# Attention and the last stage in one region, with five output blocks moved into the last stage's first slots

## Chip, core and metric
The kernel runs on one core of one Trainium2 chip. The metric is the device time of one execution in microseconds (us). Five engines with a queue each work side by side and meet at semaphores: TensorE (PE; PEld are its weight loads), VectorE (DVE), ScalarE (ACT), GpSimd (POOL) and SyncE (SP), which issues most transfers. TensorE writes its products into PSUM, eight banks of 128 x 512 floats, which the other engines empty.

## What is computed
One inference step of a decoder layer with three groups of heads, for a prompt of 1024 tokens and 8 sequences of 4 new tokens (32 rows). All is float32. Cut to what matters:

```python
def mix_out(x, a, b, c, w_out, g_post):
    hcat = concatenate([a, b, c])              # 1024 + 512 + 512 columns
    return x + rmsnorm(hcat @ w_out, g_post)

def layer(...):
    pp = split(rmsnorm(x_p, g_pre) @ w_in)
    a_p, pC, pn, pm = mlstm_branch(pp, ...)    # chunks in order, state C, n, m carried on
    b_p = sparse_attention(pp)                 # 256 keys per query, softmax, * silu(z)
    c_p = memory_attention(pp)                 # 256 memory tokens, softmax, * silu(z)
    y_p = mix_out(x_p, a_p, b_p, c_p, w_out, g_post)
    # the same for the 32 decode rows, with caches and an mLSTM state per sequence
```

The output projection `hcat @ w_out` is split by rows of `w_out`: the half of groups B and C (rows 1024 to 2047) is computed in the attention stage and stored as a partial result, the half of group A is added in the last stage.

## The kernel before
The program is four stages in order (`build`): `project_index`, `select`, `attend_bc` and `mix_out`. Each runs through `Program.run`: a region (`nc.Block`) in which each engine has its own hand-written instruction list, closed by a barrier of all engines, and then a short region in which SyncE clears the stage's semaphores.

`attend_bc` runs over units, one per tile of 128 tokens (8) and head (4): 32 units, `A_UNITS`, unit `s` in slot `s`. A slot holds the scores of one unit, the softmax of it on VectorE and ScalarE, the transposed weights and the product with the values of the unit before. Six slots behind (`A_LAG`) come the output blocks: group `n` is one of the four blocks of 512 columns of tile `n // 4` of the B and C half, eight products of 128 x 512 accumulated in the one bank `at_bank_bc` (`multiply`, L2113, its first four products ahead of `turn_h`, its last four behind). ScalarE copies the bank to SBUF (`evacuate`, L2272), SyncE stores it to `y_part` (L1963). With 32 units and a lag of 6 the slots run to 38: in slots 34 to 37 there is only a group (28 to 31) in each. After them come 32 products for the decode rows (L2211), their copy and their store (L2000). SyncE asks in slot 33 for what the last stage begins with (gate rows, decode queries and keys, units 0 and 1), in slot 34 for two blocks of `w_out` and unit 2, in slot 35 for unit 3.

`mix_out` first turns gate rows into columns (L3133), decode queries and keys (L3150), and forms the decode dots (L3157). Then slots -2 to 36 follow, one per unit (chunk of 128 tokens and head, 32 in all). In slot `s` TensorE turns the keys of unit `s + 2` (L3044), forms the dots of `s + 1` (L3054), turns the output of `s - 1` (L3090), works on a decode step (L3118, every fourth slot L3125), then the numerator of unit `s` (L3066, L3068) and its key-value products (L3079). Between these stand, five slots behind (`LAG`), two halves of four products each of an output block of group A (`multiply`, L3093; products L3105). Dots and numerator share a bank, so the dots of a unit wait until VectorE has read the numerator before (`output`, L2702); that needs a square on ScalarE (L2881) and a root on GpSimd (L2968, L2971). `w_out` blocks 2 and 3 of the A half are requested by GpSimd in slot 0 (L2989). Units are loaded by SyncE four slots ahead (`units.load`, six requests), each when the unit before it in its buffer is used up.

## Time and profile before

| | us |
|---|---|
| median of 3 runs (2821.35 to 2826.67) | 2823.8 |
| profiled execution | 2823.03 |
| its span, first to last instruction | 2821.2 |
| TensorE busy | 2722.3 (96%) |
| VectorE, ScalarE, GpSimd busy | 1249.4, 579.0, 404.7 |
| mean granted clock of TensorE | 0.985 of full |
| end of the last decode product of attention | 2407.9 |
| first instruction of the last stage on TensorE | 2411.7 |
| first output product of group A | 2471.0 |

Times in the trace count from the start of the span. A timeline row is a run of equal instructions of one engine in order of time; in brackets stands how long the engine idled before it and what ended that. A float32 product of TensorE leaves two records (a block of eight products reads x16). The end of a matmul is modelled, so rows of TensorE overlap by a few tenths; distances are taken from start to start. A table of stretches gives the busy time of each engine in a window, the mean granted clock (1.00 is 2.4 GHz, 0.50 is 1.2 GHz), the mean busy share of the DMA engines and what they moved. "DMA to landing" is the time from a request to its arrival.

### The profile page before, as it was taken

What the parts mean: (1) busy time and instruction counts of PE and PEld (TensorE: products, weight loads), DVE (VectorE), ACT (ScalarE), POOL (GpSimd) and SP (SyncE); (2) the same over time, 40 slices, a digit from 0 to 9 for tenths busy, and PEclk for the clock granted to TensorE, in tenths of its full rate; (3) what the DMA queues carried; (4) which work ended last, traced back from release to release, by engine and by line L of the source; (5) the groups of instructions that cost most, each with busy time, mean ns of one, the idle gap of its engine ahead of it and who ended that gap; (6) DMA issues with size and microseconds to landing.
All of it is one profiled execution on the core that took longest, in us unless ns stands there. A gap on an engine that the chain in (4) does not pass through costs nothing. (4 is left out here: it accounts for less than half of the span.)

```text
span 2821.2 us, 35962 instructions
## 1 busy us (share of the span) xinstructions
PE 2722.3 (96%) x13915; PEld 1935.7 (69%) x13915; DVE 1249.4 (44%) x2147; ACT 579.0 (21%) x1367; POOL 404.7 (14%) x819
## 2 busy tenths in 40 slices
PE   8998999999999999999999999999699999699998
PEld 6674468846844588888888888888455564455553
DVE  3252588767754572142222245441322331345453
ACT  3123458660000000000011100110222231122121
POOL 0000013320000000000000033220133100334332
PEclk9999999999999999999999999999899999799999
DMA  6458212211322221222332255443945214665652
GB/s 228 103 158 269 84 36 72 84 44 59 103 75 84 68 79 43 74 83 85 105 122 76 84 179 158 136 137 113 306 142 155 79 47 136 206 198 178 209 156 99
DMA packets 273463, 342.00 MB, mean 121 GB/s; under 512 B 40989, under 2 KB 226325, under 8 KB 268013
## 3 DMA queue, kind: packets, MB, share of 16 engines
q1 hardware_dynamic: 239932, 262.65, 29.7%
q0 software_dynamic: 16288, 67.46, 7.6%
q10 hardware_dynamic: 17072, 9.58, 1.1%
q8 instruction: 112, 1.84, 0.3%
q14 instruction: 59, 0.48, 0.1%
HBM read 262.16 MB, written 80.01 MB: 121 GB/s over the span
## 5 line engine op out<-in xcount | busy, mean ns | idle before, releaser
L1396 PE MATMUL sbank<-w,xT 128*128 128x256 f32 x3200 | 698.6, 379 | 0.0
L1396 PEld LDWEIGHTS sbank<-w,xT 128*128 128x128 f32 x3200 | 606.5, 190 | 85.0 <-issue 3.3
L1396 PE MATMUL sbank<-w,area 128*128 128x256 f32 x1664 | 361.3, 379 | 0.0
L1815 DVE TENSOR_TENSOR pout_b<-pout_b,sbank 128x256 f32<-128x256 f32 x320 | 134.3, 421 | 503.4 <-PE sbank L1396 414.7
L1396 PEld LDWEIGHTS sbank<-w,area 128*128 128x128 f32 x1664 | 315.9, 190 | 42.8
L1778 DVE TENSOR_TENSOR w<-w 128x2048 f32<-128x2048 f32 x63 | 142.9, 2289 | 320.6 <-PE sbank L1396 257.4
L2121 PE MATMUL at_bank_bc<-w,at_hT 128*128 128x512 f32 x512 | 229.9, 593 | 3.9 <-ACT at_bc_out L2276 3.9
L1488 ACT ACTIVATE pout_b<-sbank 128x256 f32<-128x256 f32 x120 | 45.1, 382 | 890.6 <-PE sbank L1396 658.3
L1396 PE MATMUL sbank<-w 128*128 128x256 f32 x832 | 181.8, 379 | 2.6 <-issue 2.6
L1396 PEld LDWEIGHTS sbank<-w 128*128 128x128 f32 x832 | 158.0, 190 | 24.2 <-issue 2.8
L1393 PE MATMUL sbank<-xT,w 128*128 128x512 f32 x384 | 166.6, 593 | 0.0
L2121 PEld LDWEIGHTS at_bank_bc<-w,at_hT 128*128 128x128 f32 x512 | 94.6, 190 | 103.0 <-issue 101.6
L1393 PEld LDWEIGHTS sbank<-xT,w 128*128 128x128 f32 x384 | 72.7, 190 | 90.1 <-issue 90.0
L3105 PE MATMUL mo_bank_acc<-area,w 128*128 128x512 f32 x256 | 116.2, 598 | 0.0
L3105 PE MATMUL mo_bank_acc<-w 128*128 128x512 f32 x256 | 116.2, 598 | 0.0
L1512 ACT ACTIVATE pout_b<-pout_b 128x256 f32<-128x256 f32 x72 | 30.0, 417 | 358.9 <-DVE pout_b L1815 358.9
L2012 POOL DMA_INDIRECT at_vg<-in_cache_v,rowid x64 | 60.5, 945 | 277.6 <-PE at_bank_dec L2174 148.3
L1393 PE MATMUL sbank<-area,w 128*128 128x512 f32 x192 | 82.9, 592 | 0.0
L3105 PEld LDWEIGHTS mo_bank_acc<-area,w 128*128 128x128 f32 x256 | 46.4, 190 | 52.6 <-issue 52.6
L3105 PEld LDWEIGHTS mo_bank_acc<-w 128*128 128x128 f32 x256 | 46.5, 190 | 52.1 <-issue 52.0
L1596 DVE MAX8 m8s<-decode_scores 128x8 f32<-128x2052 f32 x32 | 73.4, 2294 | 0.1
L1599 DVE FIND_INDEX8 c8s<-m8s,decode_scores 128x8 uint32<-128x2052 f32 x32 | 73.3, 2291 | 0.0
(446 smaller groups left out, 3295.7 us busy)
## 6 DMA issues: line engine op xcount, KB each, us to landing
w<-in_w_in SPq DMA_DIRECT2D x64, 1024.0 KB, 5.1
proj<-pout_b SPq DMA_DIRECT2D x208, 128.0 KB, 1.7
area<-in_x_prompt SPq DMA_DIRECT2D x16, 1024.0 KB, 7.6
attention_then_units<-proj SPq DMA_DIRECT2D x128, 128.0 KB, 2.6
area<-roped_q_of_decode POOLq DMA_DIRECT2D x32, 256.0 KB, 4.1
w<-in_w_out SPq DMA_DIRECT2D x4, 2048.0 KB, 15.5
y_of_groups_b_c<-at_bc_out SPq DMA_DIRECT2D x32, 256.0 KB, 2.3
mo_dec_states<-in_state_mlstm_C SPq DMA_DIRECT2D x32, 256.0 KB, 6.4
```

The lines of the kernel that those rows point to most:

```text
L1393: last = nc.tensor.matmul(bank[2 * u][:, :], at[name][:, c, P * u:P * (u + 1)], x(c, 0, SEQ // 2), start=first_ and c == 0, stop=c == 7, s ...
L1396: last = nc.tensor.matmul(bank[t][:, 0:256], x(c, t * P, (t + 1) * P), at[name][:, c, :], start=first_ and c == 0, stop=c == 7, skip_group ...
L1488: nc.scalar.activation(out[:, t, :], product_at(n, t), function if kind else ACT.Copy).then_inc(first_read, 1)
L1512: nc.scalar.activation(qout[:, t, :], qout[:, t, :], function).then_inc(shaped, 1)
L1596: order.step(nc.vector.max(m8s[:], ss[:]))
L1599: order.step(nc.vector.max_index(c8s[:], m8s[:], ss[:]))
L1778: nc.vector.tensor_tensor(quarter[out], quarter[x], quarter[y], op).then_inc(w_sums, 1)
L1815: nc.vector.tensor_tensor(out[:, t, :], x[:, t, :], product_at(n, t), ALU.add).then_inc(sums_read, 1)
L2012: nc.gpsimd.indirect_dma_start(out=vg[:, 4 * (q % 2) + g, :], out_offset=None, in_=ins["cache_v"][:, :], in_offset=bass.IndirectOffsetOnAx ...
L2121: last = nc.tensor.matmul(acc[:, :], hT[:, t % 2, j, :], w[:, j, b * O_W:(b + 1) * O_W], start=j == 0, stop=j == HT - 1)
L3105: last = nc.tensor.matmul(acc[n % 2][:, :], hT[:, c % 2, j, :], w[b][:, j, :], start=j == 0, stop=j == HT - 1)
```

## The change
Attention and the last stage run in one region, `run_joined`. Each engine goes from its attention list straight on to its list of the last stage, where it first waits for one semaphore, `attention_over` (`over`). SyncE raises it after its last wait of attention and after clearing attention's semaphores. The semaphores that both stages use are kept in the program's outer list.

Attention keeps 28 groups (`BC_OWN`), the tiles 0 to 6. The last of them goes into the bank `at_bank_dots0` instead of the shared one. The five blocks that are left (`BC_CARRIED`): the decode block (`None`) and block 3 of tile 7 stand at the end of attention's list, into the banks `kept_bank1` and `kept_bank0`; blocks 2, 0 and 1 of tile 7 come in slots -1 and 0, 1 and 2, 3 and 4 of the last stage, two products ahead of and two behind the dots of a slot (`carry`). The kept banks are the later banks of the A half. ScalarE copies the carried blocks (`copy_carried`), SyncE stores them (`store_carried`), with waits for the landing of the store that used the buffer before.

For that, the transposed outputs of odd tiles, of the decode rows and the two output buffers live over both stages; `w_out` lies in four separate blocks; gate columns and decode dots go to the bank `th`; the normalizer of the decode rows is asked for by attention; the load of `w_out` block 0 and 1 and of units 2 and 3 moves behind the start of the last stage; GpSimd's blocks 2 and 3 move to slots 3 and 5, since they overwrite the B and C half.

```diff
+    def run_joined(self, first, second):
+        with ExitStack() as second_stage:
+            with self.nc.Block() as joined:
+                with ExitStack() as self.stage:
+                    self.in_stage = []
+                    first(self, joined)
+                self.stage, self.in_stage = second_stage, []
+                second(self, joined)
...
+BC_OWN = A_UNITS - O_B
+BC_CARRIED = (None, O_B - 1, 2, 0, 1)
...
-        slots = range(A_UNITS + A_LAG)
+        slots = range(A_UNITS + 2)
+        def out_bank(n):
+            return qs0 if n == BC_OWN - 1 else acc
...
         @block.sync     # attention
-                if s == A_UNITS + 2:
-                    for b in range(2):
-                        sp.dma_start(k.w_a(b), ins["w_out"][0:ML_W, b * O_W:(b + 1) * O_W].rearrange("(c p) n -> p c n", p=P)
-                                     ).then_inc(k.w_a_in[b], 16)
-                    units.load(sp, 2)
-                if s == A_UNITS + 3:
-                    units.load(sp, 3)
-            n = A_UNITS - 1
+            n = BC_OWN - 1
             sp.wait_ge(evacuated, n + 1)
-            sp.wait_ge(evacuated, A_UNITS + 1)
-            sp.dma_start(k.y_part_dec[:, :], out[:, 0, :]).then_inc(y_out[0], 16)
-            sp.wait_ge(y_out[0], 16 * (A_UNITS // 2 + 1))
-            sp.wait_ge(y_out[1], 16 * (A_UNITS // 2))
+            k.clear(sp)
+            sp.sem_inc(k.attention_over, 1)
...
         @block.tensor   # attention
-                    if n:
+                    if n == BC_OWN - 1:
+                        pe.wait_ge(read, A_UNITS)
+                    elif n:
                         pe.wait_ge(evacuated, n)
...
-            pe.wait_ge(evacuated, A_UNITS)
+            pe.wait_ge(evacuated, BC_OWN - 1)
             for c in range(HT):
                 for b in range(O_B):
...
+            pe.wait_ge(h_kept, A_UNITS)
+            b = BC_CARRIED[1]
+            for j in range(HT):
+                last = nc.tensor.matmul(ov[:, :], k.hT_odd[:, j, :], w[b][:, j, :], start=j == 0, stop=j == HT - 1)
...
         @block.sync     # last stage
+            def store_carried(i):
+                b = BC_CARRIED[i]
+                sp.wait_ge(bc_copied, copied(i))
+                sp.dma_start(k.y_part_dec[:, :] if b is None else k.y_part[SEQ - P:SEQ, O_W * b:O_W * (b + 1)],
+                             k.out_parts[:, i % 2, :]).then_inc(y_part_out[i % 2], 16)
...
+            units.load(sp, 2)
+            store_carried(0)
+            for j in range(ML_H):
+                load_states(j)
+            units.load(sp, 3)
+            load_w(0)
+            store_carried(1)
+            load_w(1)
+            for j in range(ML_H, 8):
+                load_states(j)
             for s in slots:
+                if s in (1, 3, 5):
+                    store_carried(2 + s // 2)
...
         @block.scalar   # last stage
+            def copy_carried(i):
+                act.wait_ge(bc_done, copied(i))
+                act.wait_ge(y_part_out[i % 2], 16 * (BC_OWN + i) // 2 if i % 2 == 0 else 16 * (BC_OWN + i - 1) // 2)
+                nc.scalar.activation(k.out_parts[:, i % 2, :], carried_bank(i)[:, :], ACT.Copy).then_inc(bc_copied, 1)
...
+                if s == -2:
+                    copy_carried(1)
+                if s in (0, 2, 4):
+                    copy_carried(2 + s // 2)
...
         @block.gpsimd   # last stage
-                if s == 0:
-                    for b in range(2, O_B):
+                if s in (3, 5):
+                    b = 2 + s // 5
+                    pool.wait_ge(bc_done, copied(b + 1))
...
         @block.tensor   # last stage
+            def carry(s, part):
+                i, first = carried(s), 4 * ((s + 1) % 2) + 2 * part
+                if first == 0:
+                    pe.wait_ge(bc_copied, copied(i - 2))
+                for j in range(first, first + 2):
+                    last = nc.tensor.matmul(carried_bank(i)[:, :], k.hT_odd[:, j, :], w_bc[BC_CARRIED[i]][:, j, :],
+                                            start=j == 0, stop=j == HT - 1)
+                if first == HT - 2:
+                    last.then_inc(bc_done, 1)
```

What stands in TensorE's list at the junction, before. `at_hT` are the turned head outputs, `at_dec_hT` those of the decode rows, 32 x 512 their products.

```order
L2121 MATMUL at_bank_bc<-w,at_hT 128x512 x8
L2133 MATMUL at_bank_turn<-ident_sb,at_ho 128x128 x2
L2121 MATMUL at_bank_bc<-w,at_hT 128x512 x36
L2211 MATMUL at_bank_bc<-w,at_dec_hT 32x512 x32
L1864 UNCONDITIONAL_BRANCH
L3037 UNCONDITIONAL_BRANCH
```

And now, with both banks called `kept_bank`.

```order
L2154 MATMUL kept_bank<-w,at_hT_of_even_tiles 128x512 x4
L2154 MATMUL at_bank_dots<-w,at_hT_of_even_tiles 128x512 x4
L2166 MATMUL at_bank_turn<-ident_sb,at_ho 128x128 x2
L2154 MATMUL at_bank_dots<-w,at_hT_of_even_tiles 128x512 x4
L2244 MATMUL kept_bank<-w,dec_hT 32x512 x32
L2250 MATMUL kept_bank<-w,hT_of_odd_tiles 128x512 x8
L3134 UNCONDITIONAL_BRANCH
```

The 36 products in a row (half of group 27, then groups 28 to 31) are gone from in front of the decode block; eight of them stand behind it, and one branch to the next list is left of two.

The opening of the last stage on TensorE, from the decode dots to the turn after the first numerator, before.

```order
L3157 MATMUL mo_bank_acc<-mo_dec_qT,mo_dec_kT 32x32 x8
L3054 MATMUL mo_bank_dots_num<-attention_then_units,mo_kT 128x128 x2
L3044 MATMUL mo_bank_turn_qk<-ident_sb,attention_then_units 128x128 x2
L3054 MATMUL mo_bank_dots_num<-attention_then_units,mo_kT 128x128 x2
L3066 MATMUL mo_bank_dots_num<-attention_then_units,mo_sd 128x257
L3068 MATMUL mo_bank_dots_num<-mo_state,mo_qs 128x257 x2
L3079 MATMUL mo_bank_kv<-attention_then_units,mo_kw 128x257 x2
L3196 MATMUL mo_bank_dec_num<-mo_dec_v,mo_dec_sd 32x257 x4
L3044 MATMUL mo_bank_turn_qk<-ident_sb,attention_then_units 128x128 x2
```

And now, `hT_of_odd_tiles` being the carried operand.

```order
L3262 MATMUL mo_bank_turn_h<-mo_dec_qT,mo_dec_kT 32x32 x8
L3210 MATMUL kept_bank<-w,hT_of_odd_tiles 128x512 x2
L3151 MATMUL mo_bank_dots_num<-attention_then_units,mo_kT 128x128 x2
L3210 MATMUL kept_bank<-w,hT_of_odd_tiles 128x512 x2
L3141 MATMUL mo_bank_turn_qk<-ident_sb,attention_then_units 128x128 x2
L3210 MATMUL kept_bank<-w,hT_of_odd_tiles 128x512 x2
L3151 MATMUL mo_bank_dots_num<-attention_then_units,mo_kT 128x128 x2
L3210 MATMUL kept_bank<-w,hT_of_odd_tiles 128x512 x2
L3163 MATMUL mo_bank_dots_num<-attention_then_units,mo_sd 128x257
L3165 MATMUL mo_bank_dots_num<-mo_state,mo_qs 128x257 x2
L3176 MATMUL mo_bank_kv<-attention_then_units,mo_kw 128x257 x2
L3305 MATMUL mo_bank_dec_num<-mo_dec_v,mo_dec_sd 32x257 x4
L3141 MATMUL mo_bank_turn_qk<-ident_sb,attention_then_units 128x128 x2
```

Four pairs of products of the first carried block came in around the dots (L3054, now L3151), all ahead of the first numerator (L3066, now L3163).

SyncE's list before, from the store of group 27 on: the `w_out` blocks and unit 2.

```order
L2485 DMA attention_then_units<-gate_rows 128x2x128
L1963 DMA y_of_groups_b_c<-at_bc_out 128x512
L1991 DMA area<-in_w_out 128x8x512 x2
L2480 DMA attention_then_units<-mlstm_queries_turned 128x2x128
L2483 DMA attention_then_units<-proj 128x256 x3
L2484 DMA attention_then_units<-proj 128x256
L2485 DMA attention_then_units<-gate_rows 128x2x128
```

And now, from the last request of unit 1 on (the ISA row are the clears, with the release right behind them).

```order
L2522 DMA attention_then_units<-gate_rows 128x2x128
L130 ISA x9
L2032 DMA y_of_groups_b_c<-out_parts 128x512
L2630 UNCONDITIONAL_BRANCH
L2648 DMA mo_dec_rows_everywhere<-gate_rows 128x8x32
L2650 DMA mo_decay_everywhere<-gate_decay 128x64
L2652 DMA mo_dec_mask<-in_dec_causal 32x32
L2654 DMA mo_dec_row_of<-in_dec_row_of 32x8 x2
L2656 DMA mo_dec_v<-proj 32x4x256 x2
```

The release stands ahead of the constants, and no block of `w_out` stands in front of them; these follow behind unit 3.

## Rows read from the trace of the kernel before

**Rows 1.** Page, part 2: granted TensorE clock in tenths, 40 equal slices of the span.
```profile
PEclk9999999999999999999999999999899999799999
```

**Rows 2.** Table of stretches: window, length, busy PE, PEld, DVE, ACT, POOL; clock, DMA, GB/s.
```profile
2407.90:2428.40 20.50, 8.00 (x59) 6.27 (x59) 9.49 (x25) 3.35 (x12) 8.12 (x16) 0.62 0.60 173
2428.40:2449.10 20.70, 14.85 (x68) 9.33 (x68) 7.23 (x23) 3.64 (x11) 8.02 (x17) 0.75 0.98 346
2449.10:2471.00 21.90, 17.95 (x59) 13.16 (x58) 11.25 (x40) 3.92 (x12) 5.89 (x13) 0.66 0.61 184
...
2480.40:2534.90 54.50, 54.50 (x207) 30.88 (x206) 27.85 (x79) 11.71 (x35) 21.33 (x36) 1.00 0.64 186
```

**Rows 3.** Timeline of TensorE: start, length, line, operation, output<-inputs, count, [idle before <-releaser].
```profile
2364.88 3.60 PE L2121 MATMUL at_bank_bc<-w,at_hT 128*128 128x512 f32 x8
2369.26 7.11 PE L2121 MATMUL at_bank_bc<-w,at_hT 128*128 128x512 f32 x16 [0.78 <-ACT at_bc_out L2276]
...
2400.79 7.07 PE L2211 MATMUL at_bank_bc<-w,at_dec_hT 128*32 128x512 f32 x64 [0.78 <-ACT at_bc_out L2276]
2411.74 0.66 PE L3133 MATMUL mo_bank_acc<-ident_sb,attention_then_units 12*128 12x12 f32 x9 [3.88 <-PEq L113]
```

**Rows 4.** Timeline of VectorE, same columns.
```profile
2412.20 1.77 DVE L2770 MEMSET mo_state<- 128x2056 f32 x1 [54.81 <-PEq L113]
...
2420.23 0.42 DVE L2680 TENSOR_TENSOR mo_qs<-attention_then_units 128x256 f32<-128x256 f32 x1 [3.80 <-DMA mo_dec_row_of<-in_dec_row_of]
...
2422.21 0.28 DVE L2689 SCALAR_TENSOR_TENSOR mo_sd<-mo_bank_dots_num,mo_dt 128x128 f32<-128x128 f32 x1
...
2456.45 0.29 DVE L2689 SCALAR_TENSOR_TENSOR mo_sd<-mo_bank_dots_num,mo_dt 128x128 f32<-128x128 f32 x1 [0.54 <-PE mo_bank_dots_num L3054]
```

**Rows 5.** Timeline of TensorE, opening and first slots of the last stage.
```profile
2416.48 1.06 PE L3157 MATMUL mo_bank_acc<-mo_dec_qT,mo_dec_kT 128*32 128x32 f32 x16 [0.23 <-DVE mo_dec_kT L2783]
...
2428.43 1.20 PE L3066 MATMUL mo_bank_dots_num<-attention_then_units,mo_sd 128*128 128x257 f32 x2 [4.61 <-DVE mo_sd L2689]
...
2446.46 0.44 PE L3044 MATMUL mo_bank_turn_qk<-ident_sb,attention_then_units 128*128 128x128 f32 x2 [4.88 <-DMA attention_then_units<-gate_rows]
...
2450.16 1.92 PE L3068 MATMUL mo_bank_dots_num<-mo_state,mo_qs 128*128 128x257 f32 x4
...
2455.73 0.68 PE L3054 MATMUL mo_bank_dots_num<-attention_then_units,mo_kT 128*128 128x128 f32 x4 [1.68 <-DVE mo_a L2709]
...
2470.99 3.60 PE L3105 MATMUL mo_bank_acc<-area,w 128*128 128x512 f32 x8
...
2475.81 1.08 PE L3125 MATMUL mo_bank_dec_num<-mo_dec_states,mo_dec_q_slot 128*32 128x257 f32 x16
```

**Rows 6.** Timeline of SyncE's requests (SPq) at attention's end.
```profile
2368.49 0.43 SPq L2485 DMA_DIRECT2D attention_then_units<-gate_rows  x1
...
2370.87 7.23 SPq L2480 DMA_DIRECT2D attention_then_units<-mlstm_queries_turned  x1
```

**Rows 7.** Timeline of TensorE, one steady slot.
```profile
2480.36 0.60 PE L3066 MATMUL mo_bank_dots_num<-attention_then_units,mo_sd 128*128 128x257 f32 x2
2480.79 1.03 PE L3068 MATMUL mo_bank_dots_num<-mo_state,mo_qs 128*128 128x257 f32 x4
...
2482.74 3.60 PE L3105 MATMUL mo_bank_acc<-area,w 128*128 128x512 f32 x8
2486.18 0.61 PE L3054 MATMUL mo_bank_dots_num<-attention_then_units,mo_kT 128*128 128x128 f32 x4
...
2487.57 3.70 PE L3105 MATMUL mo_bank_acc<-area,w 128*128 128x512 f32 x8
2491.11 0.60 PE L3066 MATMUL mo_bank_dots_num<-attention_then_units,mo_sd 128*128 128x257 f32 x2
```

**Rows 8.** Landing: w_out blocks (page, part 6, median), gate_rows in 2340 to 2480.
```profile
w<-in_w_out SPq DMA_DIRECT2D x4, 2048.0 KB, 15.5
...
DMA to landing us min/median/max: 3.5/5.3/11.0
```

More of the change, by code:

```diff
@@ L2489, with mix_out @@
 DEC = DEC_B * ML_H
-def mix_out(k):
+def mix_out(k, block):
     nc, ins, outs = k.nc, k.ins, k.outs
@@ L3128, in decode @@
                     last.then_inc(d_num, 1)
+            pe.wait_ge(over, 1)
             pe.wait_ge(rows_in, 16)
@@ L3162, in _ @@
                     multiply(group(s), 0)
+                if carried(s) is not None:
+                    carry(s, 0)
                 if -1 <= s and s + 1 < UNITS:
@@ L3188, in _ @@
                     multiply(group(s), 1)
+                if carried(s) is not None:
+                    carry(s, 1)
                 if 0 <= s < UNITS:
```

141 lines of the change are left out of this document (92 added, 49 removed).

## The prediction

> **What bounds the kernel now.** I read the 40 slices of the page first. TensorE's granted clock is 9 tenths or more but for two slices, of which the second covers 2398 to 2468 us [rows 1]; it lies at the junction that the change touches. The stages are serial, so what is gained at a junction comes off the end. The table of stretches sizes the dip [rows 2]: from 2407.9 to 2471.0 TensorE is busy 40.8 of 63.1 us at a mean clock of 0.62 to 0.75, so much of that busy time is itself time at 1.2 GHz. From 2480.4 to 2534.9 it is never idle, at full clock.
>
> The timeline of TensorE shows what stands there [rows 3]. The last tile's four output blocks of eight products run alone: 7.11 us each (16 records stand for 8 products, 0.86 us a product), each after a gap of 0.78 in which ScalarE empties the single bank. The decode block of 7.07 follows, then 3.88 of nothing at the barrier. VectorE does nothing meanwhile: its first work comes after 54.8 us of idling [rows 4]. Once the last stage has begun, its first numerator product starts only at 2428.43, 16.7 after TensorE came back [rows 5]. That is a latency chain: the constants land at 2420.2, only then does VectorE go on, and it takes 8.2 more. The next slots are again waits on the other engines, plus one of 4.88 for a unit's rows, with the products between them at half speed. The filler (the blocks) stands before the hole instead of in it.
>
> **Part 1: attention's end.** Group 27 goes to a bank of its own, so one gap of 0.78 goes: its second half starts at 2364.1 instead of 2364.88 and is through 3.44 later, at 2367.5. The decode block follows (7.1, to 2374.6), then block 3 of the last tile into the second kept bank (7.1, to 2381.7), without a gap, since that bank is free. Before, this point lay at 2407.87. Three blocks are put off, and a wait on one semaphore replaces the barrier.
>
> **Part 2: does TensorE find the semaphore raised?** SyncE raises it behind the last tile's requests and the two first units, which are issued by 2368.9 [rows 6]. The decode normalizer adds an issue (as the others, 0.43), and the copy of group 27 that SyncE waits for is over at about 2368.4. Nine clearing instructions follow. The whole restart in the trace, with seven of them, two barriers and a store's landing, is 3.88, so the release lies between 2369.3 and 2373.2; I take 2370.3. All of it is before 2381.7, the time TensorE gets there. From then on VectorE's fill of 1.77, the constants and GpSimd's first tables run under the decode block and block 3. The constants took from 2411.74 to 2420.23, 8.5: they are there by 2379, or by 2381.7 at the late end, still ahead of their first use at about 2388. The two w_out blocks of 2 MB and units 2 and 3 are moved behind the release; in the trace the issue right behind those blocks took 7.23 [rows 6]. That jam moves to about 2386 and ends before unit 4 is asked for at about 2398.
>
> TensorE's jump to the next code takes something between 0 and the 3.88 of the restart. I take 0.6, near the lower end, since the 3.88 also holds landing, barriers and clears. The Trainium skill (Runtime: NRT & Kernel Launch, Instruction fetch mechanics) has a rule against it: a taken branch to code that isn't at hand must fetch before execution goes on. By it the sum would lose up to 3.3 more; the trace holds such a jump in the same 3.88 and shows none by itself.
>
> **Part 3: the opening.** TensorE starts at 2382.3. In the trace it needs 4.74 from its first transposes to the decode dots (2411.74 to 2416.48) and 1.06 for these [rows 3, 5], which gives 2388.1. The first quarter of a carried block (two products, 1.72) ends at 2389.8. From the start of a unit's dots to VectorE's weights are 0.72 (2455.73 to 2456.45), and from the first weights to the first numerator 6.22 (2422.21 to 2428.43) [rows 4, 5]. So the first numerator starts at 2396.8. In the last 6.9 us TensorE has three quarters (5.2) and a turn and dots (0.66), 5.8 together: hidden, with 1.1 to spare. That is block 2, for nothing.
>
> **Part 4: slots 1 to 4.** The steady slot at full clock [rows 7]: numerator, key-value products and turn 2.38, half a block 3.44, dots, turn and decode products 1.39, half a block 3.54, together 10.75. A carried slot can't be shorter than the chain through the other engines: from the numerator's end (2450.16 + 1.92 = 2452.08) to the next dots at 2455.73 are 3.65 [rows 5]. At full clock the numerator ends 0.43 + 1.03 = 1.46 into the slot; the rest of the key-value products, the turn and a quarter (1.72) fill 2.7 of the 3.65, and about 0.9 stays idle. So a slot is 1.46 + 3.65 + 1.39 + 1.72 = 8.2. Four are 32.9, with 1.0 for the decode numerators of slot 1 (the row at 2475.81) 33.9. The fifth numerator starts at 2430.7, and 2.4 later, at 2433.1, the first output product of the stage, instead of at 2470.99. **That is 37.9 us.** Blocks 0 and 1 cost nothing: the old slots took 42.6 from the first numerator to that product (2428.43 to 2470.99), the new 36.3 with the blocks in them.
>
> ScalarE's three copies of a carried block stand ahead of a square that itself needs a numerator of 1.46; a copy fits in a gap of 0.78, so they are hidden. VectorE and GpSimd have the same work. W_out blocks 2 and 3 go out in slots 3 and 5 instead of together in slot 0; before, with both in the air, a unit's rows took up to 11.0 to land [rows 8] and stopped TensorE for 4.88 [rows 5]. With 2 MB at a time the cost of that lies between 0 and twice 4.88; I subtract half of one, 2.4. After slot 5 the program is as before, bound by TensorE at 10.75 a slot.
>
> **Sum.** 37.9 − 2.4 = 35.5. The profiled execution took 2823.03 (span 2821.2), 0.8 under the median 2823.8 of the runs: 2823.03 − 35.5 = 2787.5, given as 2787.
>
> **Rivals.**
> *The clock stays low in the carried slots.* For: 0.62 to 0.75 in the three stretches [rows 2], and after a wait of 1.68 dots at 0.68 where the steady slot has 0.61, numerator products of 1.92 where it has 1.03 [rows 5, 7]. Against: the gaps of 0.78 between blocks left the next block at 7.11, full speed [rows 3]; a carried slot has one gap of 0.9; and the first output block ran at full speed at once after slots that were mostly busy. At half speed throughout, TensorE's 5.8 of the opening become 11.6 and its dots come later (numerator at 2404), a slot is 2 × (2.38 + 1.72 + 1.39 + 1.72) = 14.4, and the first output product comes at 2468.5: 2.5 gained, 2821. With half of it low, 2803. The Trainium skill (TensorE: Matmul & The Clock Gate, HAM oscillation — how this bites in real kernels) says that waits between short bursts put the engine back to half rate each time anew. The trace agrees for its long waits and not for 0.78; by the rule in every slot the time would be this rival's.
>
> *Units' rows land late.* SyncE requests some 8 MB from 2370 to 2400 (two blocks of 2048 KB, eight states of 256 KB, two units, two stores), and 346 GB/s at a share of 0.98 was the stretch that held the stall [rows 2]. If each of slots 2 to 5 waits 4.88, 19.5 of the 37.9 go: 2805. Two such waits give 2795. Against: unit 4 has from 2398 to about 2407.
>
> *The release comes late.* If SyncE's queue holds it until TensorE is through block 3, the constants cost their 8.5 behind it: 2796. Against: only small requests stand ahead of it in the order.
>
> *Slower.* Each of the three carried copies waits for the landing of the store two before it, and these stores stand in SyncE's queue among the w_out blocks (median 15.5 to land [rows 8]). ScalarE works in order, so a late landing holds the next unit's square, and that holds TensorE. Three times 15.5 is 46.5 against 37.9 gained: 2832. It decides from 12.6 a copy on. Against: the first such store goes out at about 2385 and is wanted at 2412.
>
> **Chances.** Forecast 0.69 (2780 to 2795), clock 0.10, late rows 0.13, late release 0.05, slower 0.03. Below: no stall may stay (2.4) and the idle 0.9 of four slots may be less, down to 2782, and the median may sit some us off: 2779. Above I go to 2802, which leaves out the worse half of the clock rival, the worst of late rows, and the slower case. A change under 0.2%, 5.6 us, can't be told from none: faster 0.93, same 0.04 (the full clock rival), slower 0.03.
>
> **What would show it.** Right: the decode block ends near 2374.6; TensorE's first transposes for the last stage start near 2382.3; VectorE's fill of 1.77 stands at about 2370; the first numerator starts near 2397, the fifth near 2431, the first output product near 2433, at a clock of 1.0 in most of 2397 to 2433. Wrong in a step: carried products 1.7 apart instead of 0.86 (clock); TensorE waiting for gate_rows in slots 2 to 5 (late rows); waits of TensorE that end with a copy of ScalarE (slower). The forecast as a whole is wrong if the slots after 5 grow beyond 10.75.

## The result and the profile after

The changed kernel takes 2790.3 us (median of 4 runs, 2788.8 to 2792.4), before 2824.5 beside it: ratio 0.988, 95% interval 0.9863 to 0.9897. Forecast were 2787 and a range of 2779 to 2802. In a second batch it took 2792.6 (2790.0 to 2797.2) against 2825.1: 0.989 [0.9875, 0.9905]. Its profiled execution took 2791.27, span 2789.4, with TensorE busy for 2710.3 us (97%) at a mean clock of 0.989.

The page's row of the granted clock, against [rows 1]: the slice of 7 at the junction is gone.

```profile
PEclk9999999999999999999999999999899999999999
```

The table of stretches, against [rows 2] (length, busy PE, PEld, DVE, ACT, POOL, clock, DMA share, GB/s).

```profile
2367.50:2381.70 14.20, 14.20 (x89) 5.35 (x81) 1.82 (x4) 0.84 (x2) 1.69 (x6) 1.00 0.85 236
2390.00:2400.00 10.00, 9.82 (x42) 5.28 (x41) 4.36 (x18) 2.63 (x7) 2.04 (x5) 1.00 1.05 393
2400.00:2410.00 10.00, 7.57 (x43) 4.57 (x43) 3.96 (x13) 1.38 (x5) 3.42 (x7) 0.93 1.03 346
2420.00:2430.00 10.00, 6.05 (x26) 4.00 (x27) 4.87 (x16) 1.36 (x4) 3.00 (x7) 0.96 1.03 352
2480.00:2534.90 54.90, 54.90 (x221) 30.97 (x221) 30.09 (x80) 11.76 (x35) 21.90 (x37) 1.00 0.60 183
```

The stretch with the decode block and block 3 has no idle time. From 2390 to 2410 and from 2420 to 2430 the DMA engines are at a share of 1.0 and more, and in the last two of these stretches TensorE is busy for 7.6 and 6.1 of 10 us. From 2480 on it is never idle, as before.

The timeline of TensorE at the junction, against [rows 3, 5]: end of attention, first turns, decode dots, first carried quarter, first numerator.

```profile
2367.03 4.50 PE L2244 MATMUL kept_bank<-w,dec_hT 128*32 128x512 f32 x40
...
2380.58 0.59 PE L2250 MATMUL kept_bank<-w,hT_of_odd_tiles 128*128 128x512 f32 x1
2381.10 0.69 PE L3239 MATMUL mo_bank_turn_h<-ident_sb,attention_then_units 12*128 12x12 f32 x9
...
2384.28 0.73 PE L3262 MATMUL mo_bank_turn_h<-mo_dec_qT,mo_dec_kT 128*32 128x32 f32 x16 [0.48 <-DVE mo_dec_kT L2864]
2384.94 3.59 PE L3210 MATMUL kept_bank<-w,hT_of_odd_tiles 128*128 128x512 f32 x4
2388.37 0.61 PE L3151 MATMUL mo_bank_dots_num<-attention_then_units,mo_kT 128*128 128x128 f32 x4
2388.81 1.88 PE L3210 MATMUL kept_bank<-w,hT_of_odd_tiles 128*128 128x512 f32 x4
...
2394.63 0.60 PE L3163 MATMUL mo_bank_dots_num<-attention_then_units,mo_sd 128*128 128x257 f32 x2
```

There is no gap between the last product of attention (L2250) and the first turn of the last stage (L3239). A quarter of a carried block is two products, four records. It takes 3.59 just behind the small turns and 1.88 one step later: the first carried quarter ran at half clock, the others of the opening at full. From the decode dots to the first numerator TensorE has no idle time.

The same timeline from slot 2 to the start of slot 5. The length of slot `s` is the distance from the numerator (L3163) of unit `s - 1` to that of unit `s`. The numerators of units 0 to 4 start at 2394.63, 2404.09, 2415.64, 2424.05 and 2436.24.

```profile
2408.85 0.69 PE L3141 MATMUL mo_bank_turn_qk<-ident_sb,attention_then_units 128*128 128x128 f32 x2 [2.43 <-DMA attention_then_units<-gate_rows]
2409.33 3.26 PE L3210 MATMUL kept_bank<-w,hT_of_odd_tiles 128*128 128x512 f32 x4
...
2420.77 0.68 PE L3151 MATMUL mo_bank_dots_num<-attention_then_units,mo_kT 128*128 128x128 f32 x4 [0.86 <-DVE mo_a L2789]
...
2429.57 0.69 PE L3141 MATMUL mo_bank_turn_qk<-ident_sb,attention_then_units 128*128 128x128 f32 x2 [3.18 <-DMA attention_then_units<-gate_rows]
2430.05 3.15 PE L3210 MATMUL kept_bank<-w,hT_of_odd_tiles 128*128 128x512 f32 x4
...
2436.24 0.60 PE L3163 MATMUL mo_bank_dots_num<-attention_then_units,mo_sd 128*128 128x257 f32 x2
...
2438.62 1.88 PE L3200 MATMUL kept_bank<-area,w 128*128 128x512 f32 x4
```

Slot 3 has no wait but the 0.86 behind VectorE and is 8.41 long. Slots 2 and 4 wait for the rows of units 4 and 6 (2.43 and 3.18), and a quarter at half clock follows each time (3.26 and 3.15 instead of 1.88). These slots are 11.55 and 12.19 long. The first output product starts at 2438.62, before at 2470.99 [rows 5].

VectorE's first instruction and SyncE's requests, against [rows 4, 6]; then GpSimd's request for `w_out` block 2.

```profile
2370.16 1.77 DVE L2851 MEMSET mo_state<- 128x2056 f32 x1 [13.14 <-SPq L130]
```
```profile
2385.18 1.27 SPq L2663 DMA_DIRECT2D area<-in_w_out  x1
2386.49 9.56 SPq L2659 DMA_DIRECT2D mo_dec_states<-in_state_mlstm_C  x4
2397.00 0.37 SPq L2517 DMA_DIRECT2D attention_then_units<-mlstm_queries_turned  x1
...
2400.12 0.64 SPq L2522 DMA_DIRECT2D attention_then_units<-gate_rows  x1
...
2421.76 0.48 SPq L2522 DMA_DIRECT2D attention_then_units<-gate_rows  x1
```
```profile
2416.10 1.00 POOL L3085 DMA_DIRECT2D w<-in_w_out  x1 [5.00 <-PE kept_bank L3210]
```

VectorE is released by SyncE's clear (L130), long before TensorE comes. Unit 4's last request goes out at 2400.12 and TensorE goes on at 2408.85; unit 6's at 2421.76, 5.7 behind 2 MB of `w_out`, and TensorE goes on at 2429.57.

### The profile page after: what moved, and what is told of

It reads as the page before. It is cut to its first block and busy times, and to the rows that moved or that the text cites. A ratio compares the mean times of both kernels' runs of the same rounds, so it can differ in the third digit from the quotient of the medians.

```text
span 2789.4 us, 35948 instructions
## 1 busy us (share of the span) xinstructions
PE 2710.3 (97%) x13915; PEld 1927.5 (69%) x13915; DVE 1244.9 (45%) x2147; ACT 580.6 (21%) x1367; POOL 404.6 (15%) x819
## 5 line engine op out<-in xcount | busy, mean ns | idle before, releaser
L3200 PE MATMUL kept_bank<-area,w 128*128 128x512 f32 x256 | 116.2, 598 | 0.0
L3200 PE MATMUL kept_bank<-w 128*128 128x512 f32 x256 | 116.2, 598 | 0.0
L2154 PE MATMUL kept_bank<-w,at_hT_of_even_tiles 128*128 128x512 f32 x240 | 107.9, 592 | 0.0
L2154 PE MATMUL kept_bank<-w,hT_of_odd_tiles 128*128 128x512 f32 x192 | 86.3, 592 | 0.0
L3200 PEld LDWEIGHTS kept_bank<-area,w 128*128 128x128 f32 x256 | 46.4, 190 | 52.6 <-issue 52.6
L3200 PEld LDWEIGHTS kept_bank<-w 128*128 128x128 f32 x256 | 46.5, 190 | 52.1 <-issue 52.0
L2154 PEld LDWEIGHTS kept_bank<-w,at_hT_of_even_tiles 128*128 128x128 f32 x240 | 44.4, 190 | 43.8 <-issue 43.0
```

The source lines that it names most:

```text
L2154: last = nc.tensor.matmul(out_bank(n)[:, :], hT[t % 2][:, j, :], w[b][:, j, :], start=j == 0, stop=j == HT - 1)
L3200: last = nc.tensor.matmul(acc[n % 2][:, :], hT[:, c % 2, j, :], w[b][:, j, :], start=j == 0, stop=j == HT - 1)
```

## The experiments

The stages before the junction, which no edit touches, differ from one profiled execution to the next: the first group product of attention starts between 2043.7 and 2058.5. So beside the times I give distances inside the profiled execution, start to start on TensorE: A from the first group product of attention to the first numerator of the last stage, B from there to the first output product, C from there to the last numerator. They come from one execution of each kernel. Each ratio is against executions of the kernel before in the same batch as the run (medians 2824.5 to 2826.2).

| run | median us (range, runs) | ratio to before, 95% | A | B | C | A+B+C |
|---|---|---|---|---|---|---|
| before | 2824.5 (2821.4 to 2826.7, 4) | | 381.23 | 42.56 | 294.86 | 718.65 |
| changed | 2790.3 (2788.8 to 2792.4, 4) | 0.988 [0.9863, 0.9897] | 347.80 | 43.99 | 294.90 | 686.69 |
| e0 | 2792.6 (2790.0 to 2797.2, 4) | 0.989 [0.9875, 0.9905] | 347.80 | 40.49 | 294.43 | 682.72 |
| e1 | 2803.6 (2800.0 to 2808.3, 6) | 0.9923 [0.9904, 0.9941] | 364.07 | 39.82 | 294.72 | 698.61 |
| e2 | 2800.6 (2797.7 to 2803.1, 6) | 0.9908 [0.989, 0.9926] | 351.63 | 49.35 | 294.67 | 695.65 |
| e5 | 2795.1 (2794.1 to 2802.2, 5) | 0.9889 [0.987, 0.9909] | 347.85 | 42.36 | 295.74 | 685.95 |
| e6 | 2789.4 (2787.6 to 2797.5, 5) | 0.9876 [0.9854, 0.9899] | 347.80 | 39.53 | 294.90 | 682.23 |
| e8 | 2790.9 (2788.5 to 2792.1, 4) | 0.9876 [0.9861, 0.9891] | 347.83 | 42.35 | 294.60 | 684.78 |
| e9 | 2794.1 (2791.9 to 2795.9, 4) | 0.9888 [0.9873, 0.9904] | 347.85 | 43.01 | 297.13 | 687.99 |
| e10 | 2802.1 (2797.0 to 2805.6, 5) | 0.9919 [0.9906, 0.9933] | 347.84 | 46.69 | 295.39 | 689.92 |
| e11 | 2791.5 (2788.2 to 2801.4, 6) | 0.9891 [0.9874, 0.9907] | 347.81 | 40.54 | 294.96 | 683.31 |
| e12 | 2792.6 (2785.2 to 2800.7, 5) | 0.9882 [0.9863, 0.9901] | 347.78 | 42.01 | 294.63 | 684.42 |
| e13 | 2792.2 (2788.7 to 2799.5, 5) | 0.9891 [0.9877, 0.9905] | 347.81 | 40.34 | 296.14 | 684.29 |
| e15 | 2803.6 (2801.0 to 2805.5, 6) | 0.9926 [0.9914, 0.9938] | 348.44 | 38.43 | 306.84 | 693.71 |

### e1: all five blocks at attention's end
The joined region stays. The three blocks of the last stage's slots move to the end of attention's list, and their copies and stores move with them, ahead of `w_out` block 0.
```diff
             last.then_inc(bc_done, 1)
+            for i in range(2, 5):
+                pe.wait_ge(evacuated, BC_OWN + i - 1)
+                for j in range(HT):
+                    last = nc.tensor.matmul((acc, ov)[i % 2][:, :], k.hT_odd[:, j, :], w[BC_CARRIED[i]][:, j, :], ...)
...
-            return 2 + (s + 1) // 2 if -1 <= s < LAG else None
+            return None
```


> The joined region stays, but all five blocks stand at attention's end, none in the slots of the last stage. Theory (filler and early start each carry a part): the three blocks take 3 x 7.0 us ahead of the last stage, so TensorE starts it at 2402; the opening and slots 0 to 4 then run without filler, about as in the kernel before less its 4.88 wait, and the first output product of group A comes near 2448 instead of 2438.6: about 2800 us. Rival (the gain is the filler alone, the missing barrier gives nothing): about 2811 to 2820. Rival (the gain is the missing barrier and the early constants alone, filler nothing): as the changed kernel, 2790.

Measured: 2803.6, above the 2800 of the theory and clear of both rivals. The joined region without blocks in the last stage takes 20.0 off A+B+C (718.65 to 698.61), and carrying three blocks takes 11.9 (changed) to 15.9 (e0) more. The timeline shows the three blocks in a row, the opening without filler, and that waits for rows are there without it:

```profile
2377.88 20.76 PE L2255 MATMUL kept_bank<-w,hT_of_odd_tiles 128*128 128x512 f32 x48
2398.58 0.69 PE L3241 MATMUL mo_bank_turn_h<-ident_sb,attention_then_units 12*128 12x12 f32 x9
...
2401.76 0.69 PE L3264 MATMUL mo_bank_turn_h<-mo_dec_qT,mo_dec_kT 128*32 128x32 f32 x16 [0.48 <-DVE mo_dec_kT L2869]
...
2407.78 1.20 PE L3165 MATMUL mo_bank_dots_num<-attention_then_units,mo_sd 128*128 128x257 f32 x2 [2.52 <-DVE mo_sd L2774]
...
2440.44 0.69 PE L3143 MATMUL mo_bank_turn_qk<-ident_sb,attention_then_units 128*128 128x128 f32 x2 [5.84 <-DMA attention_then_units<-gate_rows]
```

The 20.0 are not the missing barrier alone. The kernel before has six gaps of 0.78 behind ScalarE's copies from 2361 to 2401, which two banks in turn take away (4.7). The restart of 3.9 is gone, and from the first turns to the first numerator it takes 9.2 instead of 16.7 (7.5). B is 2.7 shorter, and the blocks themselves take 6.9 apiece instead of 7.1.

The three blocks last 20.7 here, so in the changed kernel they still cost 20.7 less 11.9 to 15.9, that is 4.8 to 8.8. Of this 4.3 lies in the opening: from the decode dots to the first numerator are 6.02 here and 10.35 in the changed kernel. The filler also goes with a higher clock in the slots. From the first numerator to the first output product it is 0.77 in e1 and 0.92 in the changed kernel (table of stretches of each):

```profile
2407.80:2447.60 39.80, 29.41 (x124) 19.84 (x125) 18.16 (x61) 6.60 (x20) 14.15 (x27) 0.77 0.95 319
```
```profile
2394.60:2438.60 44.00, 37.35 (x157) 21.92 (x156) 17.50 (x60) 8.43 (x23) 14.25 (x27) 0.92 0.85 283
```

### e2: release held until block 3 is through
```diff
             k.clear(sp)
+            sp.wait_ge(bc_done, BC_OWN + 2)
             sp.sem_inc(k.attention_over, 1)
```


> SyncE raises the release of the last stage only when the decode block and block 3 are done on TensorE (2381), so that constants, VectorE's fill and units 2 and 3 no longer run under them. Theory (latency of the constants was hidden there): the constants land about 8.5 later than 2381 and the first numerator moves from 2394.6 to about 2399 to 2403; requests move back by 11 us, which lets units come late in slots 1 and 2: 2796 to 2804 us. Rival (the early release hides nothing that matters): under 2 us more, 2792 at most.

Measured: 2800.6, inside the theory's range and 10 more than the changed kernel. Only 3.8 of it is the later first numerator (A 351.63 against 347.80). The rest came behind it. All later requests of SyncE stand behind the same wait, and units' rows are late:

```profile
2422.10 0.69 PE L3142 MATMUL mo_bank_turn_qk<-ident_sb,attention_then_units 128*128 128x128 f32 x2 [9.56 <-DMA attention_then_units<-gate_rows]
```

So the early release is worth about 10 us (9.0 to 12.9 by A+B+C), and more than half of that lies behind the first numerator. The edit delays the constants and the later transfers together; what each is worth alone no run shows.

### e5: transfers spread
```diff
-            load_w(1)
-            for j in range(ML_H, 8):
-                load_states(j)
...
                     units.load(sp, s + 4)
+                if s == 0:
+                    load_w(1)
+                if s == 1:
+                    for j in range(ML_H, 8):
+                        load_states(j)
+                if s in (2, 4):
+                    b = 1 + s // 2
+                    sp.wait_ge(bc_done, copied(b + 1))
```
The last lines request `w_out` blocks 2 and 3, and GpSimd's requests are out. Besides, the partial sums of tile 0 move to slot 3 and the gains to slot 4.

> Same work, bulk transfers later: w_out block 1 goes out behind unit 4 in slot 0, states 4 to 7 behind unit 5, w_out blocks 2 and 3 from SyncE right behind units 6 and 8 instead of from GpSimd ahead of them, the partial result of tile 0 in slot 3, the gains in slot 4. Theory (the two late units of slots 2 and 4 are behind bulk data, and each costs its idle time plus the half-speed products behind it, 3.1 and 3.8 us): no wait for gate_rows in slots 1 to 4, first output product near 2432, 2783 to 2785 us. Rival (the DMA engines are full in the whole stretch, the data only moves): waits come in other slots, 2789 to 2792.

Measured: slots 1 to 4 are 9.46, 8.40, 8.40 and 8.41 long, with no wait that lengthens them (rows hold slot 3 for 0.79, in place of the 0.86 behind VectorE). Slot 5 is 18.42 instead of 11.75:

```profile
2448.20 0.69 PE L3143 MATMUL mo_bank_turn_qk<-ident_sb,attention_then_units 128*128 128x128 f32 x2 [4.88 <-DMA attention_then_units<-gate_rows]
```

The wait went one slot on. Slots 1 to 5 sum to 53.09, in the changed kernel to 53.36. The rival holds, and with 2795.1 the time is even above its 2789 to 2792.

### e6: carried blocks in halves in slots 0, 1 and 2
```diff
-            return 2 + (s + 1) // 2 if -1 <= s < LAG else None
+            return 2 + s if 0 <= s < 3 else None
-                i, first = carried(s), 4 * ((s + 1) % 2) + 2 * part
-                for j in range(first, first + 2):
+                i, first = carried(s), 4 * part
+                for j in range(first, first + 4):
```


> The three carried blocks go in halves into slots 0, 1 and 2 (four products ahead of the dots and four behind) instead of quarters in slots -1 to 4. Theory (a slot is the longer of the chain through the other engines, 6.5, and TensorE's work): slots 1 and 2 take 10.7, slots 3 and 4 6.5 with 2.5 idle each, which also costs clock; against 8.4 for each of the four: 1 to 5 us more, with the late unit of slot 2 gone (3.1 less) and the one of slot 4 kept: 2788 to 2793. Rival (quarters matter a lot, each slot without filler falls to half clock and takes 9 or more): 2795 or more.

Measured: 2789.4, slots 12.47, 11.29, 6.59, 6.68, 11.86. The long slots leave no idle time behind VectorE, the short ones have more of it:

```profile
2426.14 0.68 PE L3151 MATMUL mo_bank_dots_num<-attention_then_units,mo_kT 128*128 128x128 f32 x4 [2.58 <-DVE mo_a L2789]
...
2431.48 0.44 PE L3141 MATMUL mo_bank_turn_qk<-ident_sb,attention_then_units 128*128 128x128 f32 x2 [1.44 <-DMA attention_then_units<-gate_rows]
```

By A+B+C it is 4.5 better than one execution of the changed kernel and 0.5 better than the other; by the intervals the two can't be told apart.

### e0: the changed kernel again


> The changed kernel once more, as the yardstick for the three beside it. Both theories expect 2790 (2787 to 2794), and in the trace two waits of TensorE for gate_rows, in slots 2 and 4 (2.4 and 3.2 us long, 3.1 and 3.8 with the half clock behind them), the five distances from numerator to numerator summing to about 53.4 where 46.4 would be free of waits. If the waits are chance of one execution, they stand elsewhere or are missing here.

Measured: the waits stand in slots 2, 3 and 4, with 0.70, 1.40 and 3.76, and the slots are 9.46, 8.42, 8.93 and 11.30 long.

```profile
2418.97 0.44 PE L3141 MATMUL mo_bank_turn_qk<-ident_sb,attention_then_units 128*128 128x128 f32 x2 [1.40 <-DMA attention_then_units<-gate_rows]
2419.24 1.88 PE L3210 MATMUL kept_bank<-w,hT_of_odd_tiles 128*128 128x512 f32 x4
...
2430.26 0.44 PE L3141 MATMUL mo_bank_turn_qk<-ident_sb,attention_then_units 128*128 128x128 f32 x2 [3.76 <-DMA attention_then_units<-gate_rows]
2430.54 1.88 PE L3210 MATMUL kept_bank<-w,hT_of_odd_tiles 128*128 128x512 f32 x4
```

So the wait in slot 4 is no chance of one execution, that in slot 2 varies. And the price of a wait can be read: a slot is longer than 8.41 by the wait less the 0.86 that the slot idles anyway (1.40 − 0.86 = 0.54, measured 0.52; 3.76 − 0.86 = 2.90, measured 2.89). Here the quarters behind ran at full clock (1.88); where they take 3.26, as in slot 2 of the changed kernel, 1.6 come on top (11.55 − 8.41 = 3.14 = 1.57 + 1.57).

### e8: no loads of w_out blocks 2 and 3
This kernel leaves out the two loads, and its output blocks 2 and 3 use `w_out` blocks 0 and 1 again.
```diff
-                if s in (3, 5):
-                    b = 2 + s // 5
...
-        w = [k.w_a(0), k.w_a(1), w_late[:, 0, :, :], w_late[:, 1, :, :]]
+        w = [k.w_a(0), k.w_a(1), k.w_a(0), k.w_a(1)]
```


> The changed kernel without the two loads of 2 MB that GpSimd asks for in slots 3 and 5: the last stage's column blocks 2 and 3 use w_out blocks 0 and 1 again, so that part of the output is not the layer's. Theory A, the late rows of slot 4 come from a queue of too much data on the DMA engines: w_out block 2 is asked for just before unit 6, so the wait of slot 4 goes (3.8) and that of slot 2 stays (3.1, behind w_out block 1 and the states): 2786.5 against 2790.3, the distances summing to 49.6. Rival B, units' rows land late because SyncE comes to their request late, whatever the load: both waits stay, 2790.

Measured: slots 3 and 4 are 8.40 and 8.40, in their stretch the DMA share is 0.59. Slot 2 is 13.70:

```profile
2412.65 0.69 PE L3136 MATMUL mo_bank_turn_qk<-ident_sb,attention_then_units 128*128 128x128 f32 x2 [3.40 <-DMA attention_then_units<-gate_rows]
2413.13 3.62 PE L3205 MATMUL kept_bank<-w,hT_of_odd_tiles 128*128 128x512 f32 x4
```

Theory A holds for slot 4: its wait comes from block 2 of `w_out` in the air ahead of unit 6. The wait of slot 2 has another cause, ahead of slot 3, and costs 5.3 here (2.54 of waiting, the rest half clock), which is why the time did not fall. Slot 2 waits longer here than in the changed kernel, although up to there the requests are the same.

### e9, e10: more spreading, in quarters and in halves
```diff
                     units.load(sp, s + 4)
+                if s in (2, 5):
+                    b = 2 + s // 5
...
-                if s == 5:
+                if s == 7:
                     sp.wait_ge(cols_turned, 1)
                     load_part(1)
```
The first lines move the requests of blocks 2 and 3, which in e5 stand in slots 2 and 4, the last ones the partial sums of tile 1. Both kernels have e5's other edits; e10 also has e6's.

> Quarters as in the changed kernel; the transfers that are not needed at once are spread: w_out block 1 behind unit 4, states 4 to 7 behind unit 5, block 2 in slot 2, block 3 in slot 5, constants for the output in slots 3, 4 and 7, all requested by SyncE behind the unit of that slot. If the wait is for order in the queue alone, no wait is left: distances sum to 46.4, 7 less than in the changed kernel, 2783. If the slots of 8.4 us are too short for what must come in them (the DMA engines were at shares of 1.0 there), a wait of about 5 comes up one or two slots later, as with the first spreading: 2788 to 2792, within 3 of the changed kernel.

> The same spreading with the three carried blocks in halves in slots 0 to 2, so that slots 3 and 4 are short (6.6). Halves alone summed to 48.9 in five distances with 2.6 us of waits, 1.4 of them for gate_rows. If spreading takes late rows away: 47.5, that is 2784 to 2786. If the short slots make the DMA engines the bound, waits of several us for gate_rows come in slots 3 to 5, and it is no better than the halves alone: 2788 to 2791.

Measured: e9 has slots of 9.46, 8.41, 8.64, 8.42 and then 20.15, with the second outcome's wait, and behind it half an output block that takes 6.30 instead of 3.60:

```profile
2439.82 0.69 PE L3143 MATMUL mo_bank_turn_qk<-ident_sb,attention_then_units 128*128 128x128 f32 x2 [5.26 <-DMA attention_then_units<-gate_rows]
2440.30 6.30 PE L3202 MATMUL kept_bank<-area,w 128*128 128x512 f32 x8
```

e10 is worse than I had for either theory: slots 12.47, 10.75, 7.82, 8.80, 16.22, of which 2.56, 2.12 (behind VectorE) and 1.92 (gate_rows) are idle. Its stretch 2430 to 2450 has a clock of 0.67 to 0.75. In both C is longer too (297.1 and 295.4 against 294.9), so spreading lengthened later slots as well. Dots behind the idle 2.56 took 1.19 instead of 0.61: here half clock also stands behind a wait for VectorE.

### e11, e12, e13: w_out blocks 0 and 1 requested in attention
```diff
+                if s == A_UNITS:
+                    sp.wait_ge(dotted, A_UNITS)
+                    sp.dma_start(k.w_a(0), ...).then_inc(k.w_a_in[0], 16)
                 if s == A_UNITS + 1:
                     sp.wait_ge(finished, A_UNITS)
                     sp.wait_ge(m_finished, A_UNITS)
+                    sp.dma_start(k.w_a(1), ...).then_inc(k.w_a_in[1], 16)
...
-            load_w(0)
             store_carried(1)
-            load_w(1)
```
e12 adds e6's halves, e13 adds e9's spreading.

> The changed kernel with w_out blocks 0 and 1 of the A half requested in attention, block 0 behind the last scores (slot 32, at about 2343), block 1 behind the last unit (about 2358), where the DMA engines stand at shares under 0.1, instead of at 2383 and 2385. Theory A (the waits of slots 2 and 4 are the DMA engines catching up with what is asked for from 2370 on): 4 MB less at 2383 to 2400, the 9.5 us in which SyncE's queue stands behind block 1 gone, unit 4 lands in time: no wait in slot 2, that of slot 4 at most half: distances sum to 46.4 to 48.5 where the changed kernel has 49.9 to 53.4, 2784 to 2787. Rival B (requests for a unit come too late in slots of 8.4 us however empty the engines are): both waits stay, 2790 to 2792. A third: the blocks delay units 0 and 1 and the constants, and the first numerator comes later than 10.4 behind the decode dots.

> The same early blocks, with the three carried blocks in halves in slots 0, 1 and 2. Halves alone had distances that sum to 48.9 with 1.4 of waits for gate_rows and 2.6 for the clock and VectorE; if the engines' backlog is gone they sum to 45.5 to 47.5, so 2784 to 2787, as good as e11 or 1 better. If the short slots 3 and 4 (6.6 us) now ask for more than lands, 2788 to 2790.

> The early blocks and quarters, and besides the states 4 to 7 behind unit 5, w_out block 2 in slot 2 and block 3 in slot 5 from SyncE behind the unit of the slot, constants in slots 3, 4 and 7. Spreading without early blocks ended in a wait of 5.3 in slot 5. If that was the sum of the data, 4 MB less of it leave no wait: distances sum to 46.4, 2783 to 2785. If it is block 2 or 3 in the air that holds a unit's rows whatever went before, one wait of 2 to 5 stays: 2787 to 2790.

Measured, e11: block 0 went out at 2354.33 only, behind a store in SyncE's list, and block 1 at 2364.57, yet the first numerator is not later (A 347.81). Slot 2 is free of waits (8.44), slots 3 and 4 still wait:

```profile
2419.81 0.44 PE L3145 MATMUL mo_bank_turn_qk<-ident_sb,attention_then_units 128*128 128x128 f32 x2 [1.47 <-DMA attention_then_units<-gate_rows]
...
2431.07 0.44 PE L3145 MATMUL mo_bank_turn_qk<-ident_sb,attention_then_units 128*128 128x128 f32 x2 [3.72 <-DMA attention_then_units<-gate_rows]
```

The sum of slots 1 to 5 is 49.90, in e0 49.86: neither theory in full. The backlog of slot 2 is gone (share 0.69 from 2400 to 2410, e0 had 1.07), and it was not what costs in slot 4. e12 (12.47, 10.75, 6.60, 7.87, 13.68) has 2.58 for VectorE in slot 3 and 2.38 for rows in slot 4. e13 has slots 1 to 4 at 9.45, 8.41, 8.40, 8.42 and one long wait, in slot 5 (16.73 instead of 11.75). SyncE's requests for block 2 and for the rows of unit 7, and TensorE's wait for these:

```profile
2417.30 0.47 SPq L2736 DMA_DIRECT2D w<-in_w_out  x1
...
2427.84 0.45 SPq L2528 DMA_DIRECT2D attention_then_units<-gate_rows  x1
```
```profile
2434.32 0.44 PE L3146 MATMUL mo_bank_turn_qk<-ident_sb,attention_then_units 128*128 128x128 f32 x2 [3.06 <-DMA attention_then_units<-gate_rows]
```

It is the second case of its expectation: with less data ahead, a unit's rows are still late behind 2 MB. The time, 2792.2, is above the 2787 to 2790 given for it.

### e15: w_out blocks 2 and 3 in pieces
```diff
                     units.load(sp, s + 4)
+                for b, first, past in {3: ((2, 0, 2),), 4: ((2, 2, 4),), 5: ((2, 4, 8), (3, 0, 2)), 6: ((3, 2, 6),), 7: ((3, 6, 8),)}.get(s, ()):
+                    sp.wait_ge(bc_done, copied(b + 1))
+                    sp.dma_start(w[b][:, first:past, :], ins["w_out"][P * first:P * past, ...]...).then_inc(w_in[b], 16)
```
With e11's early blocks.

> Early blocks as in e11, quarters, and w_out blocks 2 and 3 in pieces (0.5 MB in slots 3 and 4, 1.5 in 5, 1 in 6, 0.5 in 7), each requested by SyncE behind the unit of its slot, constants for the second tile in slot 7 instead of 5. Theory A (a unit's rows are late where 2 MB went out just ahead of them, and nothing else): the only waits that e11 kept, 1.5 in slot 3 and 3.7 in slot 4, go, none comes in slots 5 to 8; the five distances sum to 46.4 to 46.8 against 49.9 in e11 and 49.9 to 53.4 in the changed kernel; from the first group product to the first output product 384 to 385 (changed kernel 391.8). Time 2784 to 2788, since earlier stages differ by some us from run to run. Rival B (the slots of 8.4 us are too short for what units, states and their stores need): waits of 2 to 5 for gate_rows stay somewhere in slots 3 to 8 and the sum over slots 0 to 7 is within 1 of e11's.

Measured: slots 9.46, 8.43, 9.75, 8.40, 11.75. The big wait of slot 4 is gone and none for rows follows, B is 38.43, the shortest of all. One of 2.21 stays in slot 3, where no piece has been requested yet. But the pieces were too late for their use: TensorE idles 0.98 ahead of output block 2 and 9.10 ahead of block 3, and C is 11.9 longer than in the changed kernel. The timelines of SyncE and of TensorE:

```profile
2478.38 0.47 SPq L2735 DMA_DIRECT2D w<-in_w_out  x1
```
```profile
2484.76 5.70 PE L3204 MATMUL kept_bank<-w 128*128 128x512 f32 x8 [9.10 <-issue]
```

SyncE's step of slot 7 waits for the key-value product of unit 7, which TensorE forms in slot 8, where output block 3 begins: I had counted one slot too few. So theory A stands for slot 4, the wait in slot 3 stays as rival B would have it, and the version as a whole lost its gain to this deadline. The first piece goes out at 2435.41, behind unit 7, where the changed kernel requests the whole block in slot 3, ahead of unit 6. So the run does not tell whether the size of the pieces or their later time took the wait away. A version with the last pieces a slot earlier was not run.

## Why the prediction was right, and where not

**Attention's end: right.** The decode block ended at 2374.0 and block 3 at 2381.1, forecast 2374.6 and 2381.7, both without a gap. The 0.78 of group 27 is gone.

**The release: right, and early.** VectorE's fill stands at 2370.16, forecast 2370. e2 shows that this is worth more than the 8.5 of constants: it also lets the transfers start. The jump, for which I took 0.6 between 0 and 3.88, cost nothing that can be seen (L2250 to L3239 without a gap); the Trainium skill's rule (Runtime: NRT & Kernel Launch, Instruction fetch mechanics), if the target had not been at hand, would have shown as idle time there, and this trace has none.

**The opening: in time, with two errors that cancel.** The first numerator starts at 2394.6, forecast 2396.8. Of the 2.2, 0.4 is the earlier start of attention in this execution: A is 33.4 shorter where I had 31.6. From first turns to decode dots took 3.2 instead of 4.7: no wait for rows (before, 0.58), and a clock of 1.00 where the kernel before had 0.61. Behind the dots two terms were wrong. The chain through the other engines, with the dots, needs 6.0 (e1), where I had 8.0 without the quarter. And TensorE's own products, which I had as hidden with 1.1 to spare, take all of the 10.35 to the numerator, the first quarter at half clock (3.43 start to start where I had 1.72). So block 2 was not for nothing, as I had said: it costs 4.3 there, against e1. That the opening still came out 1.8 early is in part luck.

**A carried slot: 8.41, forecast 8.2.** From numerator to dots 5.12 (forecast 1.46 + 3.65), the idle 0.86 (0.9), the rest 1.46 and 1.82 instead of 1.39 and 1.72. Four slots cost 0.8 more. The forecast let blocks 0 and 1 cost nothing; against e1, B is 0.7 (e0) and 4.2 (changed) longer, with other waits for rows in it.

**The term that was mis-sized: the load stalls.** I subtracted 2.4, half a stall of 4.88. The two executions show 6.9 (3.14 and 3.78 in slots 2 and 4) and 3.4. My argument against late rows was that unit 4 has from 2398 to 2407. Its requests went out from 2397.0 to 2400.8, as I had it, but TensorE wanted the rows at 2406.4 and went on with them at 2408.9. The DMA engines stood at a share of 1.0 meanwhile; that this made the rows late is argued for slot 2, and shown for slot 4 by e8. My bounds (0 to twice 4.88) held it, and "two such waits" was the rival that partly came true, at 3.1 and 3.8 apiece instead of 4.9.

**After slot 5: right.** C is 294.90 and 294.86.

**The sum.** A+B+C is 32.0 and 35.9 shorter in two executions, by medians 34.2 and 32.5, forecast 35.5. The opening gave 1.8 more than forecast. Slots and stalls took 5.3 more in the first execution (0.8 + 6.9 − 2.4; B is 43.99 where the forecast's 36.3 + 2.4 makes 38.7) and 1.8 more in the second (0.8 + 3.4 − 2.4; B is 40.49), and in the second C is 0.4 shorter: 35.5 + 1.8 − 5.3 = 32.0, and 35.5 + 1.8 − 1.8 + 0.4 = 35.9. So the gain was forecast 1.3 and 3.0 too large by the medians, and by the distances 3.5 too large and 0.4 too small. The times are 2.7 and 5.1 above 2787.5. Of this 1.4 and 2.1 come from the kernel before, whose medians are that much above the profiled execution that I started from. The stalls are the term behind it, and the opening's error stands against it. That the second execution comes within 0.4 is luck.

**The rivals.** The clock is not low in the carried slots by itself: quarters take 1.88 in slots with the gap of 0.86; in the changed kernel half speed stands only behind the small turns and behind some of the waits for rows. The Trainium skill (TensorE: Matmul & The Clock Gate, HAM oscillation — how this bites in real kernels) describes waits between bursts that put the engine back to half rate each time. The gaps of 0.86 did not do that here, the waits of 2.43 and 3.18 did, and one of 3.76 in e0 did not. Where the filler is missing (e1), the clock in the same stretch is 0.77. No wait of TensorE ends with a copy of ScalarE, so the slower case has nothing for it. A late release did not happen; made to happen in e2, it costs 10, where I had 8.5.

What stays open: why slot 2 waits 2.43, 0.70 and 3.40 in three executions (changed, e0, e8) with the same order of requests up to there, and what holds unit 5 for 1.4 to 2.2 in e0, e11 and e15. None of the variants is faster than the changed kernel by more than the intervals.

## What to carry to other kernels

Work that only needs an early operand belongs into the hole of the next stage's opening. Joining the stages, with its extra banks, gave 20 of 32 to 36 us, and the three blocks carried into the hole the rest. The filler is not free: 20.7 us of products still cost 4.8 to 8.8 where they stand. A carried slot is 8.4 us long where a steady one has 10.75, so a unit's rows have less time to land, and the next bound is the transfers: list what is in the air, in MB a slot, before moving the requests. Moving the 2 MB loads by a slot moved the wait (e5, e9, e13). Leaving them out (e8) or requesting them later in pieces (e15) took the wait of slot 4 away, but e15's last piece came too late for its use, so count the slots up to the deadline.

## What the runs showed that I had not expected

- A wait costs its length less the idle time that it replaces: in e0 1.40 cost 0.52 and 3.76 cost 2.89, with 0.86 idle per slot anyway. Whether the clock falls behind it is not told by its length: after 3.76 a quarter took 1.88, after 2.43 it took 3.26.
- The distance A is 347.78 to 347.85 in ten profiled executions of nine kernels, while the start of the same stretch moves by 12.0 us between them (2046.4 to 2058.5). So for a change that acts on A this distance tells more here than medians of five runs. That is not so for B: two executions of the changed kernel have 43.99 and 40.49.
- Four requests of 256 KB took SyncE 9.56 us to issue behind 4 MB in flight (2.03 without), and unit 4 still was requested at 2397.00, as early as its buffer allowed; what was late was its landing.
